# Gate rows of seven post-norms: two DMAs through a DRAM row in place of diagonal blocks and a ones product

## The reference, cut to what matters

```python
def modulate(x, mod, j):
    shift, scale = mod[:, 3 * j], mod[:, 3 * j + 1]
    return x * (1 + scale[:, None, :]) + shift[:, None, :]

def post_norm_update(x, y, mod, j, g, b):
    gate = mod[:, 3 * j + 2][:, None, :]
    return layer_norm(ALPHA * x + gate * y, g, b)

def half_ffn_sublayer(x, mod, j, wi, wo, g, b):
    y = 0.5 * swiglu(modulate(x, mod, j), wi, wo)
    return post_norm_update(x, y, mod, j, g, b)
```

## Time and profile before

| | |
|---|---|
| Median of 3 runs | 1706.85 us (1706.64, 1706.85, 1719.06) |
| Profiled execution, its own time | 1715.83 us |
| Its span, first to last instruction | 1714.1 us |
| Mean granted TensorE clock | 0.970 |
| Bytes moved by DMA | 345.72 MB, mean 202 GB/s |

### The profile page before, as it was taken

How to read it: one execution, slowest core, us unless ns; L and a number is a source line. 1 busy time by engine, 2 the same in 40 slices (tenths; PEclk the granted TensorE clock), 3 DMA queues, 4 the chain that set the end, 5 groups by cost and what they waited for, 6 DMA issues and landing times.

```text
span 1714.1 us, 23912 instructions
## 1 busy us (share of the span) xinstructions
PE 1616.8 (94%) x7663; PEld 1319.9 (77%) x7663; DVE 1219.1 (71%) x1899; ACT 810.9 (47%) x1256; POOL 130.3 (8%) x191
## 2 busy tenths in 40 slices
PE   6989979899889999999999798999999999989997
PEld 5877768787778888888787456887888878768876
DVE  6877888877877775777757767777477765475555
ACT  5465545556344453444544455444354443264442
POOL 1100001100001110011000010111001100000000
PEclk9999989999989999899999899999989999999999
DMA  9763549643568886588746105988568873356551
GB/s 317 263 223 108 178 148 330 227 168 103 177 206 279 276 267 206 156 280 280 238 143 211 49 22 192 289 276 266 182 204 280 276 246 123 110 160 194 177 183 59
DMA packets 199266, 345.72 MB, mean 202 GB/s; under 512 B 10852, under 2 KB 127900, under 8 KB 198668
## 3 DMA queue, kind: packets, MB, share of 16 engines
q1 hardware_dynamic: 174668, 252.90, 44.8%
q0 software_dynamic: 24512, 91.73, 16.9%
HBM read 343.54 MB, written 1.05 MB: 201 GB/s over the span
## 4 chain that ended last, share of the span: by engine, by line
PE 82%; DVE 9%; issue 4%; ACT 2%; DMA 2%; DVEq 0%; SPq 0%; ACTq 0%; POOLq 0%
PE acc L538 24%; PE acc L540 23%; PE acc L539 23%; DVE w_lo L1452 2%; DMA mod_raw<-in_mod_w 2%; PE score L662 2%; PE turn L873 1%; PE acc L774 1%; PE score L962 1%; PE score L754 1%; DVE att_work L2012 1%; PE score L861 1%; PE turn L763 1%; PE score L650 1%; DVE acc_ctx L1572 1%
## 5 line engine op out<-in xcount | busy, mean ns | idle before, releaser
L1452 DVE TENSOR_TENSOR w_lo<-raw,w_hi 128x1024 fp32r<-128x1024 f32 (+1 forms) x490 | 586.0, 1200 | 298.1 <-ACT w_hi L1077 291.7
L1077 ACT ACTIVATE w_hi<-raw 128x1024 fp32r<-128x1024 f32 (+1 forms) x490 | 508.4, 1043 | 565.9 <-PE acc L540 565.6
L538 PE MATMUL acc<-w_hi,xT_hi 128*128 128x512 f32 (+1 forms) x1456 | 588.5, 404 | 23.8 <-DVE xT_lo L1499 8.5
L540 PE MATMUL acc<-w_hi,xT_lo 128*128 128x512 f32 (+1 forms) x1456 | 574.0, 394 | 0.0
L539 PE MATMUL acc<-w_lo,xT_hi 128*128 128x512 f32 (+1 forms) x1456 | 573.3, 394 | 0.0
L538 PEld LDWEIGHTS acc<-w_hi,xT_hi 128*128 128x128 f32 x1456 | 279.1, 192 | 85.4 <-issue 26.6
L540 PEld LDWEIGHTS acc<-w_hi,xT_lo 128*128 128x128 f32 x1456 | 278.0, 191 | 59.2
L539 PEld LDWEIGHTS acc<-w_lo,xT_hi 128*128 128x128 f32 x1456 | 279.2, 192 | 55.8 <-issue 1.2
L455 POOL DMA_DIRECT2D mod_raw<-in_mod_w x144 | 104.3, 724 | 985.5 <-DVE mod_run L1572 799.4
L538 PE MATMUL acc<-w_hi,hT_hi 128*128 128x512 f32 x440 | 174.4, 396 | 0.8 <-DVE hT_lo L1920 0.8
L540 PE MATMUL acc<-w_hi,hT_lo 128*128 128x512 f32 x440 | 173.7, 395 | 0.0
(11 more groups left out here) (260 smaller groups left out, 1303.2 us busy)
## 6 DMA issues: line engine op xcount, KB each, us to landing
raw<-in_ffn_wi SPq DMA_DIRECT2D x220, 512.0 KB, 4.9
mod_raw<-in_mod_w POOLq DMA_DIRECT2D x144, 512.0 KB, 4.4
raw<-in_ffn_wo SPq DMA_DIRECT2D x110, 512.0 KB, 4.5
raw<-in_w_in SPq DMA_DIRECT2D x72, 512.0 KB, 5.4
raw<-in_w_out SPq DMA_DIRECT2D x16, 512.0 KB, 4.4
raw<-in_attn_wqkv SPq DMA_DIRECT2D x16, 512.0 KB, 4.5
wide<-in_b_merge POOLq DMA_DIRECT2D x4, 1024.0 KB, 9.5
raw<-in_w_branch_a SPq DMA_DIRECT2D x8, 512.0 KB, 4.2
```

Of the source, the lines that this page charges most:

```text
L538: nc.tensor.matmul(dst, xh, wh, start=start, stop=False)
L540: return nc.tensor.matmul(dst, xl, wh, start=False, stop=stop)
L1077: nc.scalar.activation(w_hi[:, i % SPLIT_SLOTS, 0:n], raw[:, s, i % 2 * PIECE:i % 2 * PIECE + n], ACT.Copy).then_inc(hi_ready, 1)
L1452: nc.vector.tensor_tensor(w_lo[:, i % SPLIT_SLOTS, 0:n], raw[:, i // 2 % RAW_SLOTS, i % 2 * PIECE:i % 2 * PIECE + n], w_hi[:, i % SPLIT_SL ...
```

## The change

`gate_rows` is gone from PE, DVE and ACT, and `gate_diag` with it. POOL gets `gate_load`: a DMA writes the 128 x 8 block of `mod_lat` or `mod_ctx` to a row of 1024 floats in DRAM (`gate_vectors`), so that element k*128 + p of the row comes from partition p, column k; POOL waits for it to land; a second DMA broadcasts the row to all partitions of `gate_row`. A new semaphore, `mods_ready`, tells POOL that the vectors are stored; DVE raises it with a memset of one column behind `kept_store`. The factor 0.5 moves into the multiplication in `post_norm`, which becomes a scalar_tensor_tensor. `post_norm` waits for the second DMA and not for the two copies.

```diff
+            def gate_load(mod, j, stored):
+                n = c.now("gate")
+                v = (3 * j + 2) * KD
+                pool.wait_ge(mods_ready, stored)
+                pool.dma_start(gate_vectors[n].rearrange("(k p) -> p k", p=P), mod[:, v:v + KD], allow_slow_non_contiguous=True).then_inc(gate_out, 16)
+                pool.wait_ge(gate_out, 16 * c.next("gate"))
+                pool.dma_start(gate_row[:], gate_vectors[n].partition_broadcast(P)).then_inc(gate_in, 16)
...
             mods_of(0, 2)
+            gate_load(mod_lat[:, 0, :], 0, LAYERS)
             mods_of(1, 0)
+            pool.wait_ge(x_ready, c.next("x", 2))
+            gate_load(mod_ctx, 0, LAYERS)
             pool.wait_ge(ctx_ready, 2)
             pool.dma_start(qkv_bias[:], a["attn_bqkv_2"][0].partition_broadcast(P)).then_inc(att_in, 16)
             pool.dma_start(band[:], a["band"].rearrange("(t p) n -> p t n", p=P)).then_inc(band_in, 16)
             norm_rows(a["ln_g_2"][0, 1], a["ln_b_2"][0, 1])
+            gate_load(mod_lat[:, 0, :], 1, LAYERS)
...
             mods_of(1, 1)
+            gate_load(mod_lat[:, 0, :], 2, LAYERS + 1)
             pool.wait_ge(x_ready, c.next("x", 2))
             norm_rows(a["ln_g_2"][1, 0], a["ln_b_2"][1, 0])
             mods_of(1, 2)
+            gate_load(mod_lat[:, 1, :], 0, LAYERS + 2)
             pool.wait_ge(x_ready, c.next("x", 2))
             norm_rows(a["ln_g_2"][1, 1], a["ln_b_2"][1, 1])
+            gate_load(mod_lat[:, 1, :], 1, LAYERS + 3)
             pool.wait_ge(x_ready, c.next("x", 2))
             norm_rows(a["ln_g_2"][1, 2], a["ln_b_2"][1, 2])
+            gate_load(mod_lat[:, 1, :], 2, LAYERS + 4)
...
-                pe.wait_ge(diag_ready, c.next("diag"))
-                for n in range(2):
-                    b = SCORE[n]
-                    nc.tensor.matmul(take(b)[:], ones[:], gate_diag[:, 4 * n:4 * n + 4, :], start=True, stop=True).then_inc(full[b], 1)
...
-                for n in range(2):
-                    nc.scalar.activation(gate_row[:, n * 512:n * 512 + 512], filled(SCORE[n])[:], ACT.Copy).then_inc(moved[SCORE[n]], 1)
...
+            def mods_stored():
+                nc.vector.memset(free[:, 0:1], 0.0).then_inc(mods_ready, 1)
...
-                for k in range(KD):
-                    v = (3 * j + 2) * KD + k
-                    m = nc.vector.tensor_scalar(gate_diag[:, k, :], ident[:], mod[:, v:v + 1], factor, ALU.mult, ALU.mult)
-                m.then_inc(diag_ready, 1)
...
-                dve.wait_ge(moved["score1"], c.now("gate"))
+                dve.wait_ge(gate_in, 16 * c.next("gate"))
...
-                    nc.vector.tensor_tensor(gated[:, t, at], bank[b][:], gate_row[:, at], ALU.mult).then_inc(moved[b], 1)
+                    nc.vector.scalar_tensor_tensor(out=gated[:, t, at], in0=bank[b][:], scalar=factor, in1=gate_row[:, at],
+                                                   op0=ALU.mult, op1=ALU.mult).then_inc(moved[b], 1)
```

More of the change, by code:

```diff
@@ L74 @@
 MOD_RING = 2
+N_GATES = 7
 MOD_KEPT = 3 * D // 512
@@ L136, in sem @@
             return ctx.enter_context(nc.semaphore(name))
+        gate_vectors = nc.dram_tensor("gate_vectors", (N_GATES, D), F32).ap()
         bank = {b: ctx.enter_context(nc.psum_tensor(b, [P, 512], F32)) for b in BANKS}
@@ L310, in program @@
         silu_done = sem("silu_done")
-        diag_ready = sem("diag_ready")
+        mods_ready = sem("mods_ready")
+        gate_out = sem("gate_out")
+        gate_in = sem("gate_in")
         k_twice_ready = sem("k_twice_ready")
@@ L492, in _ @@
                 nc.gpsimd.tensor_tensor(xT_lo[:, u, :], att_out[:, u % 2, :], xT_hi[:, u, :].bitcast(F32), ALU.subtract).then_inc(out_split, 1)
-            c.next("x", 2)
             pool.wait_ge(x_ready, c.next("x", 2))
@@ L1595, in kept_store @@
                 nc.vector.tensor_tensor(mod_lat[:, l, at], filled("score1")[:, 0:4 * MOD_KEPT], modb[:, l, at], ALU.add).then_inc(moved["score1"], 1)
+                mods_stored()
             split()
@@ L1848, in second_tile, with post_norm @@
                 turn_tile(1)
-            def gate_rows(mod, j, factor):
-                dve.wait_ge(moved["score1"], c.now("score1") + 1)
-                for k in range(KD):
-                    v = (3 * j + 2) * KD + k
-                    m = nc.vector.tensor_scalar(gate_diag[:, k, :], ident[:], mod[:, v:v + 1], factor, ALU.mult, ALU.mult)
-                m.then_inc(diag_ready, 1)
[L1857 to L1861, removed]
-                dve.wait_ge(moved["score1"], c.now("gate"))
+            def post_norm(x, ready, factor, last_pieces, rows=32, first_half=None, **splits):
+                dve.wait_ge(gate_in, 16 * c.next("gate"))
                 def gate(t, n):
                     at, b = slice(n * 512, n * 512 + 512), ACC[2 * n + t]
-                    nc.vector.tensor_tensor(gated[:, t, at], bank[b][:], gate_row[:, at], ALU.mult).then_inc(moved[b], 1)
+                    nc.vector.scalar_tensor_tensor(out=gated[:, t, at], in0=bank[b][:], scalar=factor, in1=gate_row[:, at],
+                                                   op0=ALU.mult, op1=ALU.mult).then_inc(moved[b], 1)
                 def add(t, n):
@@ L1939, in ffn @@
                 c.next("piece", 4 * N_FC)
-                post_norm(x, ready, KF, rows, **end)
+                post_norm(x, ready, 0.5, KF, rows, **end)
                 if mods:
@@ L1944, in attention @@
             def attention():
-                gate_rows(mod_lat[:, 0, :], 1, 1.0)
                 def landed(*banks):
@@ L2056, in attention @@
                 split(8 - LEAD)
-                post_norm(x, x_ready, 4, first_half=lambda: products(4), **by_tile)
+                post_norm(x, x_ready, 1.0, 4, first_half=lambda: products(4), **by_tile)
             def fourier():
```

11 lines of the change are left out of this document (removed).

## The result

| | before, same chip | after |
|---|---|---|
| Median of 8 runs each | 1712.33 us (1704.62 to 1720.13) | 1698.86 us (1695.80 to 1702.09) |
| Ratio | | 0.9915, 95% interval [0.9890, 0.9939] |
| Profiled execution, its own time | 1715.83 us | 1696.36 us |
| Its span | 1714.1 us | 1694.6 us |
| Mean granted TensorE clock in it | 0.970 | 0.971 |

The change made the kernel 0.85% faster: 0.0085 x 1712.3 = 14.5 us, between 10.4 and 18.8 by the interval. The forecast was 12.15 us and 1694.7 us.

The account below looks back on a forecast made before the run. PE was taken to bound the kernel, busy for 94% of the span and 82% of the chain. Savings of 8.6 us in the FFNs and 3.55 in Fourier, 12.15 together, came off the 1706.85 us median: 1694.7 us, range 1689 to 1704.

Parts of the forecast that it names:

- PE's four passes: In each of five FFNs, removing the gate's two matmuls takes 1.72 us off the chain, 8.6 us in all.
- The rival in which the feed takes over: Behind an FFN's first projection PE would wait for `w_lo`, leaving only Fourier's gain: 1703.3 us; chance 0.10.
- Fourier, 3.55 us: From DVE's last spectrum copy to the token transform, 3.60 us shrink to one 0.04 us semaphore step, saving 3.55 us.
- the sign that I set: In Fourier, the token transform was to start within 0.1 us of the last spectrum copy if the forecast was right.
- Attention, 0: In the attention the chain runs on DVE's splits and copy of q, so removing the gate saves 0; other end 1.72 us.
- DVE's blocks, ACT's copies, factor and memsets, 0: Apart from Fourier's blocks, removed blocks and copies are off the chain; the factor and seven added memsets cost nothing: 0.
- The pair of DMAs, hidden: Store and broadcast of the gate row land before its first use in every sublayer, so they cost 0.
- its price, about 15 us: Expected time for the gate row's store plus broadcast, taking single elements as nearest to the constant's short packets.
- the bounds of 9.9 and 23.4: Low and high ends, in us, for the store and broadcast; the high end prices 1024 packets on POOL's queue.
- The rooms: Time from the store's issue to the gate row's first use: 44.8 us in the first FFN, 35.6 us in Fourier.
- The clock: Rival: half-clock stretches of PE lengthen or shorten, two places giving 1689.7 to 1699.7 us; chance 0.18 beyond a few microseconds.
- the sum of 12.15: Total predicted saving in us: 8.6 from the FFNs' passes and 3.55 from the Fourier sublayer, all else 0.

Follow-up runs that it names:

- e3: The changed kernel with the Fourier sublayer's gate alone made by blocks, product and copies as before; 1702.56 us, ratio 0.9935 to the kernel before.
- e4: The changed kernel with the attention's gate alone made by blocks, product and copies as before; 1700.91 us, ratio 0.9928 to the kernel before.
- e7: The changed kernel with five DVE weight splits moved behind later copies, three in the attention, two in Fourier; 1694.0 us, ratio 0.9893 to the kernel before.
- e2: The changed kernel with DVE's 56 diagonal blocks computed at their old places, read by nobody; 1699.86 us, ratio 0.9914 to the kernel before.
- e9: The changed kernel with both products of ones (four passes) put behind the loop of each of five FFNs; 1705.4 us, ratio 0.9949 to the kernel before.
- e10: The changed kernel with a PE pause, without the passes' work, at their old place in each of five FFNs; 1708.7 us, ratio 0.9980 to the kernel before.
- e6: The changed kernel with each store and broadcast done three times in a row, same values; 1762.34 us, ratio 1.0278 to the kernel before.

## Why the forecast came out as it did

**PE's four passes, 5 x 1.72 = 8.6 us: right.** They are gone from the chain, and e1, which puts them back there and in the Fourier sublayer (6 x 1.72 = 10.3 us on its chain), costs 8.8 ± 2.0 us at full clock and 10.3 us in the medians. The next pieces were ready as the earlier trace rows let one read: PE waits for `w_lo` nowhere in the second block. The rival in which the feed takes over falls with it: that would have given 3.6 us in all.

**Fourier, 3.55 us: right, 0.2 us too large.** 3.60 us became 0.25 and not 0.04, since "issue" there is 0.25 us; the sign that I set, a start within 0.1 us, was missed. e3 gives 3.1 us by its sublayer and 3.3 ± 1.9 by its runs. The later work did move as a whole, and the sublayer fell by 4.8 us; the other 1.4 us came ahead of the gate and were no term.

**Attention, 0: right.** The chain to the copy of q is 6.89 us after and 6.88 before; e4 changes nothing in it. The change was in a place where DVE's three splits were late anyway, and e7 shows those to be worth 3.8 us of the profile.

**DVE's blocks, ACT's copies, factor and memsets, 0: right within the runs.** e2 finds +1.6 ± 2.3 us for the blocks, and in the profile of e1, without blocks and full copies, no FFN is more than 0.2 us from before. ACT's copies were not put back alone. The factor costs nothing that shows (685 against 684 ns).

**The pair of DMAs, hidden: right; its price, about 15 us, too low.** It lasts 17 to 22 us (11.4 + 5.8 in the first FFN; 14.6 us for the attention's store alone, plus a row's 7.5), inside the bounds of 9.9 and 23.4. I took the short constant's 5.5 us as nearest, and called it 128 packets; the trace shows it as 16, of 128 bytes. The store is 16 packets too, and landed twice as late. Packets on POOL's queue rose by 1232, from 24512 to 25744; in seven pairs that is 176 each: 128 of 4 KB for the row, 16 of 256 bytes for the store, and 32 of 4 bytes. So no element is a packet of its own, and that the landing time is near the 12.1 us from 1024 packets at POOL's rate is luck: the upper bound held, by a working that the trace does not bear out. The Trainium skill's page "DMA: Bandwidth & Descriptors" would price 1024 descriptors at 10.8 us (its ≈10.5 ns a packet under "Measured", an estimate, if each were a packet): five of the seven stores landed in 10.5 to 11.6 us and two in 12.4 and 14.6, which is near it in number alone. The page has its figure from loads into SBUF and for the time in which the DMA engines are busy, and the packets shown here are through long before the landing. The rooms were 33.3 us (Fourier) and over 40 elsewhere, where I had 35.6 and 44.8.

**The clock: mis-sized as a rival, and mis-read in the base.** I expected steps of 2.5 us in two places. The profiled pair has four places of 1.7 us on the fast side and others against them, 4.9 us less in the second block and 0.8 us over the span; the runs say 1.0 ± 2.4 us on average. More weighs the base: I put the sum on the median of three runs, 1706.85 us, and said that the 9.0 us up to the profiled execution had nothing to do with what I subtract. That is right for the chain, but two of the three runs, the median among them, lie below 1712 us, in the group where the clock takes 41.5 us, and the changed kernel's runs lose 47.5. From 1706.85 the chain takes off 14.2 and the clock gives back 6.0, which is 1698.65 by these means; measured 1698.86. So the forecast time was 4.2 us too short because of its base: 6.0 us that the clock takes from the changed kernel and had not taken from the base, less the 2 us by which the gain at full clock exceeds the sum. That the two partly cancelled is luck.

**Left over:** the gain at full clock, 14.2 ± 1.7 us, is 2 us above the sum of 12.15. By the experiments more is left: e1 and e3 both hold the passes of the Fourier sublayer, so one of them has to be taken off, 14.2 - (8.8 - 1.7) - 3.3 = 3.8 us, with bounds of about ± 2.3. Blocks (e2) and attention (e4) may hold some of it by their runs, which can't tell either from zero. The profiles put none of it into the FFNs, but 2.1 us into the attention and 1.4 us into the Fourier sublayer ahead of the gate, neither of which hangs on the gate (e4, and the order on the chain). That the half clock fell differently on PE's waits there, as it does in e9 and e10, is likely and not shown.

## What to carry to other kernels

Ask of each instruction that a change takes away whether the chain of waits goes through it, and price it by the time between starts there: the passes' 1.72 us left the chain in each of five FFNs, and nothing in the attention, for the same code. A layout change by two small DMAs is free only where the vector is known long before its use; measure the room in the trace, and try the transfer doubled and trebled to see how much of it is left. And before a sum is put on a median of three runs, split each run into span x clock and the rest: differences of 10 us between runs of one kernel were the clock's. Check the split against the trace where an engine waits: in e6 and e7 it put into the clock what the chain shows as waiting.

## What the runs showed of the hardware

- A store of 128 x 8 single elements from SBUF to one row of 4 KB in DRAM landed in 10.5 to 14.6 us in the first profile of the changed kernel (9.2 to 18.8 us over all profiles), and POOL took 0.91 us to issue it, against 0.56 us for the broadcast of 512 KB. In that profile it was 16 packets of 256 bytes, and landed 6.4 to 8.5 us after the last of them.
- The broadcast of a row just written landed in 5.8 to 8.9 us, the broadcast of a constant row of the same size in 4.4 and 5.4 us (medians). They do not run at the same moments, so the cause is not shown.
- PE's stretches at 1.2 GHz at the four ends of sublayers took 1.7, 3.4 or 5.1 us each against full clock (all profiles but that of e6), and small edits in the FFNs changed one for another.
- 4.1 us more of lost clock in the first block (18.1 against 14.0 us, two profiles of one kernel) went with 0.6 us more time.
- Where PE was made to wait for DVE and a DMA (e6), the sublayers grew by 64.7 us, and the clock took 31 us more, for the most part while PE waited.
